# Expert stage of a two-layer encoder: a re-ordered head and end, and a tenth place for one early weight block

## The reference, cut to what matters

```python
def hier_moe(x, wg, bg, we, be, w_gate, w_up, w_down):
    ...
    comb = jnp.sum(jax.nn.one_hot(eid, N_EXPERTS, dtype=f32) * w[..., None], axis=-2)
    h = jax.nn.silu(jnp.einsum('bsd,edf->bsef', x, w_gate)) * jnp.einsum('bsd,edf->bsef', x, w_up)
    h = h * comb[..., None].astype(h.dtype)
    return jnp.einsum('bsef,efd->bsd', h, w_down)
...
x = x + hier_moe(rms_norm(x, norm_ffn[l]), ...)
```

## Time and profile before

| | |
|---|---|
| median of 3 runs | 1825.72 us (1822.27 to 1827.29) |
| the profiled execution: its own time, its span | 1823.12 us, 1821.1 us |
| mean granted TensorE clock | 0.992 of full speed |
| PE, PEld, DVE, ACT busy | 97%, 74%, 41%, 17% of the span |
| HBM read | 540.78 MB |
| expert stage, layer 0 and layer 1 | about 457 to 915 us and 1363 to 1818 us |

### The profile page before, as it was taken

One profiled execution on the slowest core, in us unless ns is written; L12 is line 12 of the kernel. 1 busy time (PEld: TensorE's weight loads), 2 busy tenths in 40 slices (PEclk: granted clock), 3 DMA queues, 4 the chain that ended last, 5 costly groups with the idle time before them and its releaser, 6 DMA issues.

```text
span 1821.1 us, 27222 instructions
## 1 busy us (share of the span) xinstructions
PE 1772.5 (97%) x11722; PEld 1348.6 (74%) x11722; DVE 739.1 (41%) x1553; ACT 311.2 (17%) x838; POOL 13.8 (1%) x27
## 2 busy tenths in 40 slices
PE   9999999999999999899999999999999999998998
PEld 9788887899675566655597888878995755656555
DVE  3477665676202212011235675656772111121123
ACT  3123122211210020110021231222121200202000
POOL 1000000000000000000000000000000000000000
PEclk9999999999999999999999999999999999999999
DMA  9433343547899999999884342444579999999997
GB/s 382 170 139 139 151 168 137 193 156 284 345 427 427 428 426 428 428 427 422 351 357 152 132 179 112 166 176 154 197 284 362 428 427 426 429 426 426 427 422 299
DMA packets 51434, 546.83 MB, mean 300 GB/s; under 512 B 5872, under 2 KB 6000, under 8 KB 14576
## 3 DMA queue, kind: packets, MB, share of 16 engines
q1 hardware_dynamic: 48816, 531.47, 71.0%
q0 software_dynamic: 2496, 13.57, 2.1%
HBM read 540.78 MB, written 4.24 MB: 299 GB/s over the span
## 4 chain that ended last, share of the span: by engine, by line
PE 92%; DMA 3%; SPq 2%; issue 2%; DVE 0%; DVEq 0%
PE ps L869 89%; DMA ring<-in_moe_w_down 3%; SPq L771 2%; PE ps L923 1%; PE ps L1334 0%; PE ps L1227 0%; PE ps L939 0%; PE ps L931 0%; DMA ring<-in_w_lat 0%; PE ps L1389 0%; PE ps L1022 0%; DVE ring L1925 0%; DVE v_mla L2148 0%; PE ps L1135 0%; PE ps L1108 0%
## 5 line engine op out<-in xcount | busy, mean ns | idle before, releaser
L869 PE MATMUL ps<-ring,scr 128*64 128x256 f32 (+2 forms) x2144 | 440.7, 459 | 31.6 <-issue 26.4
L869 PEld LDWEIGHTS ps<-ring,scr 128*64 128x64 f32 (+1 forms) x2144 | 211.1, 141 | 204.9 <-issue 162.4
L869 PE MATMUL ps<-ring,XN 128*128 128x256 f32 (+2 forms) x1184 | 242.2, 361 | 1.2 <-DMA ring<-in_w_lat 1.2
L869 PEld LDWEIGHTS ps<-ring,XN 128*128 128x128 f32 x1184 | 210.7, 190 | 21.7 <-issue 2.2
L869 PE MATMUL ps<-ring,X 128*128 128x256 f32 x896 | 200.6, 379 | 0.0
L869 PE MATMUL ps<-XN,ring 128*128 128x128 f32 (+1 forms) x1312 | 195.8, 306 | 0.0
L869 PEld LDWEIGHTS ps<-XN,ring 128*128 128x128 f32 x1312 | 180.3, 191 | 12.7 <-issue 3.1
L869 PEld LDWEIGHTS ps<-ring,X 128*128 128x128 f32 x896 | 169.6, 190 | 22.7
L2199 DVE TENSOR_TENSOR v_mla<-scr,ps 128x256 f32<-128x256 f32 x32 | 13.5, 421 | 347.9 <-PE ps L869 347.9
L869 PE MATMUL ps<-ring,PR 128*64 128x256 f32 x672 | 125.0, 382 | 0.0
L869 PE MATMUL ps<-PR,scr 128*64 128x256 f32 (+2 forms) x448 | 122.7, 420 | 0.0
(11 more groups left out here) (304 smaller groups left out, 2157.0 us busy)
## 6 DMA issues: line engine op xcount, KB each, us to landing
ring<-in_moe_w_gate SPq DMA_DIRECT2D x38, 2048.0 KB, 27.7
ring<-in_w_main SPq DMA_DIRECT2D x36, 2048.0 KB, 9.2
ring<-in_moe_w_down SPq DMA_DIRECT2D x32, 2048.0 KB, 30.9
ring<-in_moe_w_up SPq DMA_DIRECT2D x30, 2048.0 KB, 27.2
ring<-in_w_out_a SPq DMA_DIRECT2D x16, 1280.0 KB, 5.7
PR<-in_moe_w_up SPq DMA_DIRECT2D x10, 2048.0 KB, 29.2
XN<-in_moe_w_down SPq DMA_DIRECT2D x10, 2048.0 KB, 30.5
ring<-in_moe_w_up SPq DMA_DIRECT2D x20, 1024.0 KB, 25.9
```

Of the source, the lines that this page charges most:

```text
L869: return pe.matmul(o, lhsT, rhs, start=start, stop=stop, skip_group_check=True)
```

## The change

1. **A tenth place.** `g11_0`, the second half of the gate matrix of pair 0's second expert, no longer takes a turn in the nine places. It goes in four pieces (1 MB, 512 KB and twice 256 KB) to areas that are idle at that time (`probf`, `prf`, `bf`, `nf`), after `bc12_3`. `w_tile` finds its tiles. So ten blocks instead of nine can be requested before the first piece, `IN_PIECES` has seven names instead of eight, and the blocks behind move by one place.
2. **The first gather in two parts.** `gather(0, ..., pair)` makes the columns of one pair only: first those of pair 0 (64 of 128 columns in every matmul, so the same number of matmuls), three parts ahead of the first quarter, then two parts after the first and after the second quarter and the last after the third. Those of pair 1 follow: four parts after pair 0's `u1`, two before `dn0`, two between `dn0` and `dn1`. DVE's and ACT's copies split in the same way (`gathered(0, ..., 0)`, `gathered(1, l)`).
3. **The last pair.** Pair 6's scatters stand between the halves of `g0`, `u0`, `g1` of pair 7 instead of in `u1`, and its swept transposes (`slots_turned`) come before `u1`.
4. **The end.** The down matrices are stored in another order (four groups of 256 columns, each with its four contraction steps), so the first half of a down block is all that `dy0` needs. The last pair's `dn1` second halves come as two quarters, with a semaphore of their own (`third_in`), and `dy3` becomes two products of 256 columns, `dy3` and `dy4`. The last pair's `sc0` to `sc5` now stand between those products; two scatters follow the last one. The place of a `dn1` block of pair 7 is free at the end of `dy4`.

The diff, cut to its core:

```diff
+SCATTERED = "g11_0"
...
-    for j, name in enumerate(EXPERT):
+    for j, name in enumerate(n for n in EXPERT if n != SCATTERED):
         r.once(name, experts[j % len(experts)])
+    r.once(SCATTERED, IN_PARTS)
...
-IN_PIECES = {"dn01_0": "g0", "dn10_0": "g0", "dn11_0": "u0", "g00_1": "u0",
-             "g01_1": "g1", "u00_1": "g1", "u01_1": "u1", "g10_1": "u1"}
+IN_PIECES = {"dn10_0": "g0", "dn11_0": "g0", "g00_1": "u0", "g01_1": "u0", "u00_1": "g1", "u01_1": "u1", "g10_1": "u1"}
...
+LAST_READER.update({f"dn1{j}_{NE // 2 - 1}": f"dy4_{NE // 2 - 1}" for j in range(2)})
...
+        scattered = [(probf, 0, 2048), (prf[:, at + 1024 + SLOT:at + 2048 + SLOT], 2048, 3072), (bf[:, SLOT:SLOT + 512], 3072, 3584), (nf, 3584, SLOT)]
+
+        def w_tile(name, k):
+
+            if name != SCATTERED:
+                return slot(name)[:, k * CH:(k + 1) * CH]
+            place, lo, hi = next(part for part in scattered if part[1] <= k * CH < part[2])
+            return place[:, k * CH - lo:(k + 1) * CH - lo]
...
-                    for half in range(2):
+                    for lo, hi in ((0, 2), (2, 4)) if n != "dn1" else ((0, 2), (2, 3), (3, 4)):
                         for j in range(2):
                             name = f"{n}{j}_{NE // 2 - 1}"
-                            if half == 0:
+                            if lo == 0:
                                 sp.wait_ge(*empty(name, l))
-                            part = slice(half * (SLOT // 2), (half + 1) * (SLOT // 2))
+                            part = slice(lo * (SLOT // 4), hi * (SLOT // 4))
                             sp.dma_start(slot(name)[:, part], w[j][:, part]).then_inc(
-                                halves_in[f"{n}{j}"] if half == 0 else slot_full[SLOTS.where(name)], 16)
+                                halves_in[f"{n}{j}"] if lo == 0 else slot_full[SLOTS.where(name)] if hi == 4 else third_in[j], 16)
...
+                        sp.wait_ge(*ready(f"bc12_{N_BPAIR - 1}", l))
+                        for place, lo, hi in scattered:
+                            sp.dma_start(place, gate[l, 1, 1][:, lo:hi]).then_inc(slot_full[IN_PARTS], 16)
...
+                    cols = slice(0, QUAD * CAP_T) if pair == "" else slice(pair * CAP, (pair + 1) * CAP)
...
-                                last = mm(bank(name)[:, q * S + t * P:q * S + (t + 1) * P], xtok[:, t, d:d + P], Gm[:, t, :])
+                                last = mm(bank(name)[:, q * S + t * P + cols.start:q * S + t * P + cols.stop], xtok[:, t, d:d + P], Gm[:, t, cols])
...
-                gather(0, (0, 1))
+                gather(0, (0, 1, 2), 0)
                 for q in range(4):
-                    if q < 3:
-                        gather(0, (2 * q + 2, 2 * q + 3))
                     expert("g0", 0, (q,))
                     expert("u0", 0, (q,))
+                    gather(0, range(2 * q + 3, min(2 * q + 5, PARTS)), 0)
                 for i in range(NE // 2):
                     if i == NE // 2 - 1:
                         wait_alone(pe, *after("flags", l))
                         runs, due = sweep_due(pe)
-                    if i:
-                        expert("g0", i)
-                        expert("u0", i)
-                    expert("g1", i)
-                    turn_h(0, i)
                     if i == NE // 2 - 1:
+                        expert("g0", i, (0, 1))
                         written(i - 1)
-                        scatter(i - 1, range(KT // 4))
-                    elif gathered_in(i):
+                        scatter(i - 1, (0, 1))
+                        expert("g0", i, (2, 3))
+                        expert("u0", i, (0, 1))
+                        scatter(i - 1, (2, 3))
+                        expert("u0", i, (2, 3))
+                        expert("g1", i, (0, 1))
+                        turn_h(0, i)
+                        scatter(i - 1, (4, 5))
+                        expert("g1", i, (2, 3))
+                        scatter(i - 1, (6, 7))
+                        slots_turned(i)
+                    else:
+                        if i:
+                            expert("g0", i)
+                            expert("u0", i)
+                        expert("g1", i)
+                        turn_h(0, i)
+                    if gathered_in(i):
                         gather(gathered_in(i), range(PARTS // 2))
                     expert("u1", i)
                     if gathered_in(i):
                         gather(gathered_in(i), range(PARTS // 2, PARTS))
                     if i == 0:
+                        gather(0, range(4), 1)
                         turn_h(1, 0)
                     elif i == NE // 2 - 1:
-                        scatter(i - 1, (4, 5))
                         turn_h(1, i)
-                        scatter(i - 1, (6, 7))
                     else:
                         written(i - 1)
                         scatter(i - 1, range(KT // 4))
                         turn_h(1, i)
                         scatter(i - 1, range(KT // 4, KT // 2))
 
-                    pe.wait_ge(*freed(f"sw_{i}", l))
-                    pe.wait_ge(*after("gw", l, i))
-                    for t in range(NT):
-                        last = pe.transpose(bank(f"sw_{i}")[0:2 * CAP, t * P:(t + 1) * P], Gw[:, t, :], ident)
-                    last.then_inc(*made(f"sw_{i}"))
-
+                    if i < NE // 2 - 1:
+                        slots_turned(i)
+                    pe.wait_ge(*copied(f"ht0_{i}", l))
+
+                    def down(name, half, lo, hi):
+
+                        w = [slot(f"dn{half}{j}_{i}").rearrange("p (n k c) -> p n k c", n=4, k=4) for j in range(2)]
+                        pe.wait_ge(*freed(name, l))
+                        for k in range(4):
+                            if k == 2 and (half, lo) == (0, 0):
+                                pe.wait_ge(*copied(f"ht1_{i}", l))
+                            for j in range(2):
+                                own_rows = slice(j * CAP, (j + 1) * CAP)
+                                last = mm(bank(name)[own_rows, 0:(hi - lo) * CH], hs[:, k, own_rows], w[j][:, lo:hi, k, :], k == 0, k == 3)
+                        last.then_inc(*made(name))
+
+                    def last_blocks(half):
+                        for j in range(2):
+                            pe.wait_ge(*loaded(f"dn{half}{j}_{i}", l))
+
+                    if i == NE // 2 - 1:
+                        for j in range(2):
+                            block_in(f"dn0{j}_{i}")
+                        down(f"dy0_{i}", 0, 0, 2)
+                        last_blocks(0)
+                        down(f"dy1_{i}", 0, 2, 4)
+                        pe.wait_ge(*copied(f"sw_{i}", l))
+                        pe.wait_ge(*copied(f"dy0_{i}", l))
+                        scatter(i, (0, 1))
+                        for j in range(2):
+                            block_in(f"dn1{j}_{i}")
+                        down(f"dy2_{i}", 1, 0, 2)
+                        pe.wait_ge(*copied(f"dy1_{i}", l))
+                        scatter(i, (2, 3))
+                        for j in range(2):
+                            pe.wait_ge(third_in[j], 16 * (l + 1))
+                        down(f"dy3_{i}", 1, 2, 3)
+                        last_blocks(1)
+                        down(f"dy4_{i}", 1, 3, 4)
+                        pe.wait_ge(*copied(f"dy2_{i}", l))
+                        scatter(i, (4, 5))
+                        break
...
+                    if i == 0:
+                        gather(0, (4, 5), 1)
                     for half in range(2):
-                        pe.wait_ge(*copied(f"ht{half}_{i}", l))
-                    for half in range(2):
-                        w = [slot(f"dn{half}{j}_{i}").rearrange("p (k c) -> p k c", k=4) for j in range(2)]
+                        if half and i == 0:
+                            gather(0, (6, 7), 1)
...
+                            down(f"dy{2 * half + q}_{i}", half, 2 * q, 2 * q + 2)
...
+                for n in (3, 4):
                     pe.wait_ge(*copied(f"dy{n}_{NE // 2 - 1}", l))
-                    scatter(NE // 2 - 1, (2 * n, 2 * n + 1))
+                    scatter(NE // 2 - 1, (n + 3,))
...
-                dve.wait_ge(*ready(f"gx{n}_0", l))
+                dve.wait_ge(*ready(f"gx{n}_00", l))
                 for q in range(2):
-                    for p in range(2):
-                        k = 2 * n + q
-                        src = bank(f"gx{n}_0")[:, q * S:(q + 1) * S].rearrange("p (t a r) -> p t a r", t=NT, r=CAP_T)[:, :, 2 * p:2 * p + 2, :]
-                        ins = dve.tensor_scalar(xg(k, p).rearrange("p (j t r) -> p t j r", j=2, t=NT), src, pcol(l, R_FFN + k), None, ALU.mult)
-                ins.then_inc(*read(f"gx{n}_0"))
+                    k = 2 * n + q
+                    src = bank(f"gx{n}_00")[:, q * S:(q + 1) * S].rearrange("p (t a r) -> p t a r", t=NT, r=CAP_T)[:, :, 0:2, :]
```

(14 more changed lines are left out.)

## The result

Twenty runs of each kernel gave a median of 1828.75 us after (1820.99 to 1834.35) and 1823.24 before (1820.3 to 1827.29). The ratio is 1.0028, with an interval of 1.002 to 1.0037. Forecast were 1819.5 us and, as the range, 1812.5 to 1826; the forecast started from 1825.72, a median of three runs, so its change of −6.2 us set on the median of twenty would be 1817.0. Not only the median moved: the runs of the changed kernel spread over 13 us, those of the kernel before over 7.

The account below looks back on a forecast made before the run. Moving weight blocks bounds the expert stage's inner part, so gains lie at start, gate and end. End −6.0 and head −0.2 give −6.2 us: 1825.72 to 1819.5 us, range 1812.5 to 1826.

Parts of the forecast that it names:

- the end: Each layer's end: PE done 8.1 us after the last byte (D) instead of 11.1, 3.0 us a layer, 6.0 in all.
- the head: Start of both expert stages: gated block's bytes 1.4 us later in all, less 1.6 credit, so −0.2 us.
- the fourth rival: Head: PE's clock falls to 0.51 in the moved gather, 48 passes take 11.4 us, gate later, 1830.7 us; chance 0.08.
- 0.3 of handovers: Layer's end: 0.3 us allowed between products and scatters within the 18.0 us from `dy1` to PE's end.
- the first rival: Head: 64 columns cost half, six parts take 2.9 us, the tenth place pays, 1813.7 us; chance 0.15.
- `dn0` and the gate move by 4.7 us: Head: six gather parts (5.8 us) ahead of `dn0`, 1.1 covered by waiting, delay it and the gated block's request.
- the second gate: Pair 2's `g11_2`, waiting for pair 1's `dn0` place: request at 567.3, needed at 568.4, so no loss.
- The credit for a common restart: Behind the gate: the sixteen transfer engines begin together after a standstill, saving 0.8 us a layer (bounds 0 and 2).
- Worth nothing: Reordered first gather: first product starts 1.0 us earlier but gives it back between quarters, so `u1` ends unchanged.
- the second rival: Layer's end does not shorten: slower regrouped products or PE backlog leave it at D + 11, 1825.5 us; chance 0.18.
- third rival: Layer's end: the last quarters land late and PE waits for them, D + 11.3, 1825.9 us; chance 0.06.
- PE's lag is made up after 620 us: Pair 1 begins 6.6 us later on PE; 18.1 us of weight waits from 620 to 905 shrink by 6 or 7.

Follow-up runs that it names:

- end_alone: Only the new end (down-weight order, pair 6's scatters moved, `dy4`) on the kernel before: median 1822.99 us, ratio 1.0002.
- head_alone: Only the tenth place and the split first gather on the kernel before, with its old end: median 1832.43 us, ratio 1.0047.
- split_full: Kernel before with nine places, first gather in two parts, its passes moving all 128 columns: median 1826.42 us, ratio 1.0017.
- full_late: Changed kernel with 128-column passes in the first gather and the next layer's second and third weight tiles requested after `sc6`: 1822.15 us, ratio 0.9987.
- end_late_c1: New end alone on the kernel before, next layer's second and third weight tiles requested after `sc6` instead of `sc0`: 1818.75 us, ratio 0.998.
- no_second_full: Kernel before plus tenth place, pair 1's gather left out, pair 0's passes moving 128 columns: 1816.21 us, ratio 0.9963.
- gate_first: Changed kernel with pair 1's eight gather parts behind `dn0` (four) and `dn1` (four), none ahead of `dn0`: 1830.96 us, ratio 1.0043.
- no_second: Kernel before plus tenth place and pair 0's 64-column gather, pair 1's gather and copies left out: 1819.41 us, ratio 0.9974.
- full_columns: Changed kernel with both parts of the first gather moving all 128 columns instead of 64: 1826.02 us, ratio 1.0012.
- late_c1: Changed kernel with the next layer's second and third weight tiles requested after `sc6`: 1826.62 us, ratio 1.0013.

## Why the prediction was wrong, point by point

Two terms of the sum were mis-sized: the end, forecast at −6.0 us and measured at −0.4 (end_alone), and the head, forecast at −0.2 and measured at +9.0 (head_alone; +5.5 for the two together). In the head the step that failed is the dismissal of the fourth rival together with the doubled passes taken at 1.4 us; in the end it is the "0.3 of handovers".

- *The hole moves from the start to the gate.* Right: 292 and 275 GB/s behind the gate. *64 columns cost as much as 128:* right, 0.125 us a pass, so the first rival fell. One column per cycle, the rule of the Trainium skill ("TensorE: Matmul & The Clock Gate", section "Step-by-step: what each phase is for") that the prediction cites, does not hold for these passes.
- *"`dn0` and the gate move by 4.7 us, to 508.3 and 1412.9."* In absolute times 3.3 in layer 0 of head_alone, 5.8 and 12.5 in the profiled run, 3.6 of the last carried over from layer 0. But layer 0 of before had a fall of its own. Counted from the twelve one-column passes ahead of the gather, it looks different. PE's timeline of before, layer 1; then of head_alone, both layers, with SP's gate of layer 1; then of the change, both layers:

```profile
1356.63 1.47 PE L869 MATMUL ps<-ones,scr 128*128 128x1 f32 x12
```

```profile
450.49 1.47 PE L888 MATMUL ps<-ones,scr 128*128 128x1 f32 x12
...
1356.32 1.47 PE L888 MATMUL ps<-ones,scr 128*128 128x1 f32 x12
...
1412.69 0.33 SPq L726 DMA_DIRECT2D ring<-in_moe_w_gate  x1
```

```profile
450.33 1.47 PE L891 MATMUL ps<-ones,scr 128*128 128x1 f32 x12
...
1360.63 1.47 PE L891 MATMUL ps<-ones,scr 128*128 128x1 f32 x12
```

From these rows to the gate it took 51.6 us at the full clock before (layer 1; 53.2 in layer 0), 56.4 at the full clock with the doubled gather (head_alone, both layers), and 59.1 and 60.1 in the change. At the full clock the new head moves it by 4.8: the term was right for a clock of 1.00, and the falls add 2.7 and 3.7. The step that failed is the fourth rival's "Against it: the clock is 1.00 in every stretch from 461.5 to 503.6". Those rows came from a head whose gather is 128 columns wide; behind the 64-column one 1.2 GHz is granted in 8 heads of 12. This was the mechanism I gave 0.08, though in the first gather and first products more than in the moved parts.
- *"Head: 1.4 − 1.6 = −0.2 us."* Wrong in sign. With the clock mended the doubled passes still cost 2.8 us without the tenth place (split_full against before), and with it the head is 3.4 us slower (full_late against end_late_c1), though the tenth place brings 7.4 where nothing is doubled (no_second_full). So the doubled passes take away what the tenth place brings, and some 3 us more. I took the second gate at nothing because "it just fits". In the change it did (no hole near 568, 418 GB/s); gate_first shows that it doesn't when the first gate is freed. And I counted the 5.3 us that the queue had in hand at the gate as idle stock. In layer 0 of before the fall of the clock put the gate back by 1.6 us (53.2 against 51.6), and the transfers went on at 426 GB/s behind it. My reading, which no run tests by itself, is that the stock let the kernel before take a fall so cheaply, and that the tenth place, whose blocks come in earlier, uses it up with or without the doubled gather: the runs of no_second spread over 11.4 us, nearly as widely as the change's. The credit for a common restart could not be told apart; no run shows it.
- *"Worth nothing"* for the reordered first gather: no run has it alone. In head_alone the first product does start 1.0 us earlier at the full clock (9.1 us behind the one-column passes instead of 10.1), but the order shares the passes of 64 columns, and so the falls.
- *The end, D + 8.1.* From `dy1`'s start I had 18.0 us. The profile shows 22.6 in layer 0 and 19.2 in layer 1; end_late_c1 has 18.5 in layer 0 (`dy1` from about 893.1, PE done at 911.6). The sum of products and scatters was right to about 0.5. What it lacked is what happens between them: "0.3 of handovers" passed over a branch, and I did not ask what SP's earlier request for the next layer's tiles would collide with. That ate some 4 of the 6 us: end_late_c1 is 4.5 us faster than before, the end alone 0.4. It makes the second rival come true in layer 0, by a cause that I had not named.
- *The last quarters late (third rival):* no wait for them in either end, so nothing of the 8 us a layer either that the prediction estimated from the Trainium skill. ("DMA: Bandwidth & Descriptors", section "Anatomy of one DMA — SWDGE (gpsimd) path", gives its 2 us for transfers that GpSimd issues; these are SP's.)
- *PE's lag is made up after 620 us:*

```profile
PE ps L891 <- issue: 14.2, 7, 2.7
```

18.1 us in 11 waits before, 14.2 in 7 now: the lag is absorbed, 3.9 us of it there rather than 6 to 7.

What stays open: that narrow passes bring the clock down is shown by four pairs of kernels and by the traces, but two kernels with narrow passes (head_alone and gate_first, profiled) also went through both heads at 1.00, so it is a matter of how often, and what decides in one run isn't shown. Nor is it shown that PE's pause at the branch is the arrival of its instructions.

## What to carry to other kernels

Before filling a hole in the transfers, follow the queue to its next gate: more places help only if the work that frees them comes no later, and work doubled ahead of a gate costs twice, once in time and once, by my reading, in the stock that absorbs disturbances. A matmul whose time is set by its weights isn't made cheaper by fewer columns, and the clock may answer to it. A branch costs little until large transfers are in flight while an engine passes it: see what a step that is moved forward sets loose there.

## What the hardware showed

- The clock was at 1.2 GHz while PE was busy without a pause: 7.0 us of 7.0 at 0.51 (458 to 465), 7.4 of 7.4 at 0.54 (1368.8 to 1376.2), begun in passes of 64 columns. Short pauses had come just ahead (PE busy 6.12 us of 453 to 460 in the change), but they stood in full_columns as well (6.17), whose clock stayed at 1.00. With the same passes 128 columns wide the mean clock of the runs was higher in four kernels of four, and the first products ran at 1.00 in 16 heads of 16 instead of 4 of 12.
- A branch whose body is not entered cost PE 2.8 to 3.1 us in layer 0 with the transfers near 390 GB/s, 0.5 to 0.9 in layer 1 with them mostly idle, and in layer 0 from nothing to be seen (end_late_c1) to 0.44 us (late_c1) when the large transfers were asked for later.
